# A wider key-value product, earlier squares and reordered attention steps in a two-block transformer kernel

## The chip, the cores and the metric

The kernel runs on one core of a Trainium2 chip. The metric is the device time of one execution in microseconds (us), the median of several runs. The engines are PE (TensorE, the matmuls), PEld (its weight loads), DVE (VectorE), ACT (ScalarE), POOL (GpSimd) and SP (SyncE, which issues nearly all transfers).

## What is computed

Two transformer blocks over 256 tokens of 1024 features, all in float32. The first block mixes a gated linear attention (gla), a windowed pool and a block attention (moba), and has a feed-forward layer. The second has a feed-forward layer, a mixer, a cross attention on a memory and a second feed-forward layer. The change touches the first projection of block one and the mixer of block two:

```
proj = rmsnorm(x) @ w_in                        # block one: q, k (qk), v (gv), the gate input g1, ...
# block two, the mixer: fox attention, and NSA attention = cmp + sel + win
blocks = concat(chunks[:, i:i+nc]) + pos        # cmp: 15 blocks of 32 tokens, stride 16, per group (2) and k / v
k_cmp, v_cmp = gelu(flat(blocks) @ w1) @ w2     # 2048 -> 256 -> 64
o = g0*softmax(q k_cmp) v_cmp + g1*softmax(q k_sel) v_sel + g2*softmax(q k_win) v_win
```

## The kernel before

**Units.** All weights come from one flat array in units of at most 128 x 1024 numbers (512 KB). A chunk is a group of columns of a weight; 512 columns give 4 units of two k-tiles of 128 rows, 256 columns give 2 units of four k-tiles, and g1 with its 16 columns is one small unit. For each unit SP fetches raw (4 buffers, `fetch`), ACT rounds it to fp32r (`whi`, L1262), DVE forms the remainder (`wlo`, L1598), and PE multiplies three ways (hi*hi, lo*hi, hi*lo), 24 matmuls of 256 columns or 12 of 512. SP fetches unit u+4 when the remainder of unit u is done. A product takes its output banks from a ring of four PSUM banks when its first unit starts, and each must have been copied out by its last user; a second ring of four serves the small work. qk takes two banks, g1 one, gv two, and kv one.

**The order.** `order()` writes one plan that every engine walks through: units with their splits two units ahead (AHEAD), the ends of products (the copy out of PSUM), and the steps of tasks. After each unit there is a tick, in which every running task does one step on each engine. STEPS says how many steps a task has, THEN which task starts when another has so many steps left: sel when fox has 0 left, win when sel has 2 left. `drain` gives ticks with no unit between them, and only while the named tasks still run.

**The opening.** SP issues xT0, unit 0, xT1, unit 1, xT2, unit 2, xT3, unit 3, then the two halves of x (by tokens). ACT and DVE split the feature tiles (quarter0_n) and the units. The squares of x (squares0_0 and squares0_1, one for each half of the columns) feed the root (task rest0: sums, a power on POOL, four small DVE operations, and three ticks later `across`, which spreads the root over the partitions by a matmul and a DVE copy, rT). The ends of qk (`kept`, the two halves of gqk) and of g1 (`few`, g1T) need rT.

**The mixer of block two.** The products run qf, gf, vf, kf, kv, qn, ksw, vsw, gg0 to gg3, up10, up11, up00, up01. fox is spawned after kf, cmp after kv. fox, sel and win share `together()`, with ten steps: PE does scores (steps 1 to 3), transposes of the first token block at step 5, values(0) at step 6, the transposes of the second block (7, 8) and values(1) (9). DVE takes the peaks (1 to 3), normalises block 0 (4), at step 5 copies a bank of the transposes (`copied(0, 4)`) and normalises half of block 1, and so on. ACT has the exponentials and the other copies. moba in block one runs through the same function.

For cmp, `out_kv` at the end of kv scales the one bank [k | v] into the SBUF tile kvs. Two transfers (`across_halves`, 128 KB in all) write it with its partition halves swapped into kvx. `rows_of` then makes the tiles R[0] and R[1] (128 partitions x 16 x 32: two tokens of a block stand on the two halves of the partitions) with 8 additions of 64x240, in DVE's first three cmp steps. PE multiplies R[i] with w1 in `first_layer(i)`, L1054, at cmp's third and fourth step.

Of the kernel before, what the change touches and what calls it, by code (L numbers as in the profile page):

```python
# [11 lines left out]
ALU = mybir.AluOpType  # L12
# [5 lines left out]
T = 256  # L18
D = 1024
# [13 lines left out]
def weight_chunks():  # L33
# [16 lines left out]
    for name, a, b in (("gv", 512, 1024), ("g1", 1024, 1040), ("gr", 1040, 1552),  # L50
                       ("pu", 1552, 2064), ("mq", 2064, 2576), ("mk", 2576, 3088), ("mv", 3088, 3600)):
        add(name, "w_in", _cols((a, b)), D)
# [19 lines left out]
    add("kv", w, _cols((512, 768)), D)  # L72
# [217 lines left out]
STEPS = {"gla": 25, "pool": 5, "moba": 13, "fox": 10, "decay": 1, "cmp": 11, "sel": 10, "win": 10, "mixed_first": 1, "mixed_second": 1, "rel": 8, "memory": 16, "w1": 13,  # L290
# [11 lines left out]
THEN = {"fox": ("sel", 0), "sel": ("win", 2)}  # L302


def order(chunks, n_units):
# [9 lines left out]
    def tick():  # L315
        for name in list(left):
            yield "step", name, 0, 0
            left[name] -= 1
            n, ahead = THEN.get(name, (None, 0))
            if n and left[name] == ahead:  # L320
                spawn(n)
            if not left[name]:
                del left[name]

# [56 lines left out]

    yield from do("begin")
# [3 lines left out]
    yield from product("qk", {0: lambda: do("quarter0_3"), 1: lambda: do("squares0_0"), 2: x_squared}, open_end=True)  # L386
    yield from product("gv")
    yield "end", "qk", 0, 0
    yield from product("g1")
# [57 lines left out]
    yield from do("recall")  # L447
    yield from product("up11")
    yield from drain("cmp", "sel", "win")
# [22 lines left out]
def build(nc, io):  # L472
    with ExitStack() as ctx:
# [134 lines left out]
        kvs, kvx = m2.new("kvs", [128, 2, T]), m2.new("kvx", [128, 2, T])  # L608
# [69 lines left out]
        land["kvx"] = Landing(sem("l_kvx"), 2)  # L678
# [122 lines left out]
        def tensor(q):  # L801
# [243 lines left out]
            def cmp():  # L1045
                def first_layer(i):

                    s = ps.take("small", "cmp1", i)
                    q.wait_ge(*ps.empty("cmp1", i))
                    q.wait_ge(*land[f"w1{i}"].at())  # L1050
                    q.wait_ge(*kv_v.at("rows", i))
                    for j in range(0, 16, 4):
                        for g in range(4):
                            r = e.matmul(s[32 * g:32 * g + 32, 0:256], R[i][:, j + g, :], w1[i][:, j + g, :],  # L1054
                                         start=j == 0, stop=j == 12, tile_position=(0, 32 * g))
                    r.then_inc(*ps.filled("cmp1", i))
# [12 lines left out]
                yield  # L1069
                yield  # L1070
# [183 lines left out]
        def scalar(q):  # L1254
# [195 lines left out]
            def cmp():  # L1450
# [9 lines left out]
                yield  # L1460
                yield
# [129 lines left out]
        def vector(q):  # L1591
# [288 lines left out]
            def together(name, ready):  # L1880
# [76 lines left out]
                yield  # L1957
                if name == "sel":
                    q.wait_ge(*ps.full("cmp", "values", 1))
                copied(0, 4)  # L1960
                normalise(1, 0, slice(0, 2), 1, 0)
# [15 lines left out]
            def cmp():  # L1977
                rows_of(0, 0)
                yield
                rows_of(0, 1).then_inc(*kv_v.did("rows", 0))  # L1980
                yield
                for swapped in range(2):
                    r = rows_of(1, swapped)
                r.then_inc(*kv_v.did("rows", 1))
# [90 lines left out]
            def out_kv():  # L2075
                e.tensor_reduce(folding[:, :], ident.rearrange("p (g c) -> p c g", g=4), AX, ALU.add).then_inc(*nsa_v.did("folding"))
                for i in range(2):
                    e.memset(R[i][:, :, 30:32], 0.0)
                q.wait_ge(*used.at(ends["kv"]))
                q.wait_ge(*ps.out("across", 3))  # L2080
                e.tensor_tensor(kvs[:, :, :], ps.tile("kv", 0)[:, :].rearrange("p (i t) -> p i t", i=2), norms[3].wide(),
                                ALU.mult).then_inc(*ps.emptied("kv", 0))

            def rows_of(i, swapped):


                if swapped:
                    q.wait_ge(*land["kvx"].at())
                else:
                    q.wait_ge(*ps.out("kv", 0))  # L2090
                    q.wait_ge(*ps.out("pos"))
                for g in range(2):
                    half_ = 1 - g if swapped else g
                    pa = slice(64 * half_, 64 * half_ + 64)
                    src = (kvx if swapped else kvs)[pa, i, half_:half_ + 1]
                    windows = bass.AP(tensor=src.tensor, offset=src.offset, ap=[list(src.ap[0]), [2, 16], [16, 15]])
                    pt = posT[pa, i, :].unsqueeze(2).to_broadcast([64, 16, 15])
                    r = e.tensor_tensor(R[i][pa, :, 15 * g:15 * g + 15], windows, pt, ALU.add)
                return r
# [167 lines left out]
        def sync(q):  # L2267
# [62 lines left out]
            def across_halves():  # L2330
                q.wait_ge(*ps.out("kv", 0))
                for a, b in ((0, 64), (64, 0)):
                    load("kvx", kvx[a:a + 64, :, :], kvs[b:b + 64, :, :])
                for _ in range(10):
                    yield

# [52 lines left out]
            for i in range(4):  # L2389
                load(f"xT{i}", xT[:, 2 * i:2 * i + 2, :], io["xT"][:, 2 * i:2 * i + 2, :])  # L2390
                fetch(i)
            for t in range(2):
                load(f"x{t}", x[:, t, :], xin[:, t, :])
            load("wg2", wg2[0:16, :], io["gla_w_g2"].rearrange("a r c -> (a r) c"))
# [4 lines left out]
                tasks={"memory": memory, "moba": moba, "rel": rel_bias, "cmp": across_halves, "w1": load_w1})  # L2399
# [74 lines left out]
```

## Time and profile before

| | |
|---|---|
| median of 3 runs | 1122.28 us (1122.17 to 1125.47) |
| profiled execution | 1122.28 us, span 1120.5 us |
| PE busy | 1096.8 us, 98% of the span |
| DVE / ACT busy | 717.4 / 555.6 us |
| mean granted TensorE clock | 0.995 of full speed |
| moved by DMA | 210 MB |

The span is what the trace covers; 1.8 us of the time lie around it. In the trace a matmul's duration is modelled and overlaps the next one, so the distance of two starts is what a matmul costs. Brackets at the end of a row give the idle time of the engine before it and what ended it. L and a number is a line of the kernel.

### The profile page before, as it was taken

What the parts mean: (1) busy time and instruction counts of PE and PEld (TensorE: products, weight loads), DVE (VectorE), ACT (ScalarE), POOL (GpSimd) and SP (SyncE); (2) the same over time, 40 slices, a digit from 0 to 9 for tenths busy, and PEclk for the clock granted to TensorE, in tenths of its full rate; (3) what the DMA queues carried; (4) which work ended last, traced back from release to release, by engine and by line L of the source; (5) the groups of instructions that cost most, each with busy time, mean ns of one, the idle gap of its engine ahead of it and who ended that gap; (6) DMA issues with size and microseconds to landing.
All of it is one profiled execution on the core that took longest, in us unless ns stands there. A gap on an engine that the chain in (4) does not pass through costs nothing.

```text
span 1120.5 us, 18219 instructions
## 1 busy us (share of the span) xinstructions
PE 1096.8 (98%) x7562; PEld 986.0 (88%) x7562; DVE 717.4 (64%) x1074; ACT 555.6 (50%) x836; POOL 22.9 (2%) x43
## 2 busy tenths in 40 slices
PE   8999999999999999999999999999999999999996
PEld 8888778789999988899998899887788989999985
DVE  5686765867666645656676555767676657666653
ACT  6543575545444444544444446446645446445442
POOL 0000400000000000000000000000000000000000
PEclk9999999999999999999999999999999999999998
DMA  7544445554655655676686468233365435665661
GB/s 279 208 154 168 169 160 189 214 197 165 202 189 189 222 197 183 201 242 210 239 269 218 175 209 289 100 114 125 113 236 165 152 128 177 195 199 191 208 201 57
DMA packets 63245, 210.00 MB, mean 187 GB/s; under 512 B 7387, under 2 KB 14731, under 8 KB 62268
## 3 DMA queue, kind: packets, MB, share of 16 engines
q1 hardware_dynamic: 62876, 208.75, 55.0%
q8 instruction: 60, 0.98, 0.4%
q14 instruction: 21, 0.17, 0.0%
q10 hardware_dynamic: 288, 0.10, 0.0%
HBM read 205.39 MB, written 5.26 MB: 188 GB/s over the span
## 4 chain that ended last, share of the span: by engine, by line
PE 83%; DVE 8%; ACT 3%; issue 3%; DMA 1%; POOL 1%; SPq 0%; POOLq 0%; DVEq 0%; ACTq 0%
PE ps L835 13%; PE ps L837 13%; PE ps L838 13%; PE ps L827 12%; PE ps L829 12%; PE ps L828 12%; DVE wlo L1598 2%; PE ps L856 1%; DMA raw<-in_wflat 1%; PE ps L992 1%; DVE wlo_b L1598 1%; PE ps L978 1%; ACT whi L1262 1%; PE ps L903 1%; PE ps L1186 1%
## 5 line engine op out<-in xcount | busy, mean ns | idle before, releaser
L835 PE MATMUL ps<-hT_hi,whi_b 128*128 128x256 f32 x1376 | 383.2, 278 | 3.3 <-DVE wlo_b L1598 3.3
L837 PE MATMUL ps<-hT_hi,wlo_b 128*128 128x256 f32 x1376 | 380.4, 276 | 0.0
L838 PE MATMUL ps<-hT_lo,whi_b 128*128 128x256 f32 x1376 | 380.3, 276 | 0.0
L1598 DVE TENSOR_TENSOR wlo_b<-raw,whi_b 128x1024 fp32r<-128x1024 f32 (+1 forms) x182 | 217.1, 1212 | 109.5 <-ACT whi_b L1262 109.3
L1598 DVE TENSOR_TENSOR wlo<-raw,whi 128x1024 fp32r<-128x1024 f32 x176 | 212.5, 1224 | 116.2 <-ACT whi L1262 115.6
L835 PEld LDWEIGHTS ps<-hT_hi,whi_b 128*128 128x128 f32 x1376 | 258.7, 188 | 6.9 <-issue 5.0
L837 PEld LDWEIGHTS ps<-hT_hi,wlo_b 128*128 128x128 f32 x1376 | 258.8, 188 | 0.3
L838 PEld LDWEIGHTS ps<-hT_lo,whi_b 128*128 128x128 f32 x1376 | 258.6, 188 | 0.0
L1262 ACT ACTIVATE whi<-raw 128x1024 fp32r<-128x1024 f32 x176 | 182.0, 1056 | 112.5 <-PE ps L829 90.3
L1262 ACT ACTIVATE whi_b<-raw 128x1024 fp32r<-128x1024 f32 (+1 forms) x182 | 182.6, 1042 | 34.4 <-PE ps L829 15.5
L827 PE MATMUL ps<-whi,hT_hi 128*128 128x512 f32 (+1 forms) x256 | 101.8, 398 | 2.3 <-DVE wlo L1598 2.3
L827 PE MATMUL ps<-whi,f_hid_hi 128*128 128x512 f32 x264 | 102.8, 389 | 0.0
L828 PE MATMUL ps<-wlo,f_hid_hi 128*128 128x512 f32 x264 | 102.7, 389 | 0.0
L829 PE MATMUL ps<-whi,f_hid_lo 128*128 128x512 f32 x264 | 102.7, 389 | 0.0
L829 PE MATMUL ps<-whi,hT_lo 128*128 128x512 f32 (+1 forms) x256 | 98.2, 384 | 0.0
L828 PE MATMUL ps<-wlo,hT_hi 128*128 128x512 f32 (+1 forms) x256 | 98.2, 384 | 0.0
L1332 ACT ACTIVATE f_sg<-f_sg 128x512 f32<-128x512 f32 x33 | 20.9, 633 | 123.9 <-DVE f_sg L1741 123.9
L827 PEld LDWEIGHTS ps<-whi,hT_hi 128*128 128x128 f32 x256 | 48.1, 188 | 15.8 <-issue 3.9
L829 PEld LDWEIGHTS ps<-whi,f_hid_lo 128*128 128x128 f32 x264 | 49.6, 188 | 10.4
L827 PEld LDWEIGHTS ps<-whi,f_hid_hi 128*128 128x128 f32 x264 | 49.6, 188 | 10.2
L828 PEld LDWEIGHTS ps<-wlo,f_hid_hi 128*128 128x128 f32 x264 | 49.6, 188 | 10.1
L829 PEld LDWEIGHTS ps<-whi,hT_lo 128*128 128x128 f32 x256 | 48.1, 188 | 9.8
(324 smaller groups left out, 1263.0 us busy)
## 6 DMA issues: line engine op xcount, KB each, us to landing
raw<-in_wflat SPq DMA_DIRECT2D x356, 512.0 KB, 4.0
wide<-scratch SPq DMA_DIRECT2D x1, 2048.0 KB, 9.6
m_w<-in_cmp_k_w SPq DMA_DIRECT2D x4, 512.0 KB, 6.7
m_w<-in_cmp_v_w SPq DMA_DIRECT2D x4, 512.0 KB, 6.5
m_alibi<-in_c_alibi SPq DMA_DIRECT2D x1, 1536.0 KB, 7.3
m_xT<-in_xT SPq DMA_DIRECT2D x4, 256.0 KB, 6.6
x<-in_x SPq DMA_DIRECT2D x2, 512.0 KB, 9.8
m_memT<-in_memT SPq DMA_DIRECT2D x1, 1024.0 KB, 5.7
```

What stands on the lines that cost most here:

```text
L827: e.matmul(o, xh, hi[:, k, :], start=first and k == 0, stop=False)
L828: e.matmul(o, xh, lo[:, k, :], start=False, stop=False)
L829: r = e.matmul(o, xl, hi[:, k, :], start=False, stop=last and k == kt - 1)
L835: e.matmul(o, hi[:, k, c], xs.h(k0 + k), start=first and k == 0 and f % 2 == 0, stop=False, skip_group_check=True)
L837: e.matmul(o, lo[:, k, c], xs.h(k0 + k), start=False, stop=False, skip_group_check=True)
L838: r = e.matmul(o, hi[:, k, c], xs.l(k0 + k), start=False, stop=last and k == kt - 1, skip_group_check=True)
L856: r = e.transpose(s[:, 256 * i + 128 * t:256 * i + 128 * t + 128], src(t)[:, 128 * (f + i):128 * (f + i) + 128], ident)
L903: r = e.matmul(ss[par][:, 128 * i:128 * i + 128], kk, qq, start=True, stop=True)
L978: r = e.transpose(s[:, 128 * i:128 * i + 128], Ps[qb][:, h, 128 * k:128 * k + 128], ident)
L1262: e.activation(slot(whi, u)[:, 0:k * n], raw[u % NRAW][:, 0:k * n], ACT.Copy).then_inc(*w_hi.did(u))
L1332: e.activation(b, b, ACT.Silu).then_inc(*silu.did(i, c))
L1598: e.tensor_tensor(slot(wlo, u)[:, 0:k * n], r, h.bitcast(F32), ALU.subtract).then_inc(*w_lo.did(u))
```

## The change

- The opening: SP issues the halves of x before xT3 and unit 3. squares0_0 stands before the split of the last feature tiles, squares0_1 and the root one unit earlier. g1 is multiplied straight after qk and before gv, and the ends of g1 and then qk stand before gv.
- kv: every group of 64 columns is there twice, so kv has 512 columns, 4 units and two banks (k, v), each with both partition halves filled alike. kvs, kvx, the two transfers and rows_of go. out_kv scales each bank in place and makes 16 additions of 64x120 straight from PSUM into R. cmp has 9 steps and not 11, and PE's first layer waits for the end of out_kv's bank.
- `together()` on DVE: in step 5 the normalising comes ahead of the copy.
- win starts when sel is done, and the drain of cmp, sel and win stands before up11.

```diff
     add("qk", "w_in", _cols((256, 512), (0, 256)), D)
-    for name, a, b in (("gv", 512, 1024), ("g1", 1024, 1040), ("gr", 1040, 1552),
+    for name, a, b in (("g1", 1024, 1040), ("gv", 512, 1024), ("gr", 1040, 1552),
...
     for n in range(6):
...
     add("kf", w, _cols((1816, 2328)), D)
-    add("kv", w, _cols((512, 768)), D)
+    add("kv", w, _cols((512, 576), (512, 576), (576, 640), (576, 640),
+                       (640, 704), (640, 704), (704, 768), (704, 768)), D)
...
     add("vsw", w, _cols((896, 1024), (1152, 1280)), D)
...
-STEPS = {"gla": 25, "pool": 5, "moba": 13, "fox": 10, "decay": 1, "cmp": 11, "sel": 10, "win": 10, "mixed_first": 1, "mixed_second": 1, "rel": 8, "memory": 16, "w1": 13,
+STEPS = {"gla": 25, "pool": 5, "moba": 13, "fox": 10, "decay": 1, "cmp": 9, "sel": 10, "win": 10, "mixed_first": 1, "mixed_second": 1, "rel": 8, "memory": 16, "w1": 13,
...
     STEPS[f"rest{_i}"] = 4
...
-THEN = {"fox": ("sel", 0), "sel": ("win", 2)}
+THEN = {"fox": ("sel",), "sel": ("win",)}
...
 def order(chunks, n_units):
...
             left[name] -= 1
-            n, ahead = THEN.get(name, (None, 0))
-            if n and left[name] == ahead:
-                spawn(n)
...
                 del left[name]
+                for n in THEN.get(name, ()):
+                    spawn(n)
...
         names = names or tuple(left)
...
+    def more_x():
+        yield from do("squares0_0")
+        yield from do("quarter0_3")
...
         yield from split_to(n)
-    yield from product("qk", {0: lambda: do("quarter0_3"), 1: lambda: do("squares0_0"), 2: x_squared}, open_end=True)
+    yield from product("qk", {0: more_x, 1: x_squared}, open_end=True)
+    yield from product("g1")
+    yield "end", "qk", 0, 0
     yield from product("gv")
-    yield "end", "qk", 0, 0
-    yield from product("g1")
...
     for name in ("gr", "pu", "mq", "mk", "mv"):
...
     yield from do("recall")
+    yield from drain("cmp", "sel", "win")
     yield from product("up11")
-    yield from drain("cmp", "sel", "win")
...
     yield from product("up01")
...
         onsa = m2.new("onsa", [128, 4, T])
-        kvs, kvx = m2.new("kvs", [128, 2, T]), m2.new("kvx", [128, 2, T])
...
         folding = m2.new("folding", [128, 32], off=whi[1][2].manual_sbuf_range[1])
...
             "cv_out", "ck", "cv")}
-        land["kvx"] = Landing(sem("l_kvx"), 2)
...
                     q.wait_ge(*land[f"w1{i}"].at())
-                    q.wait_ge(*kv_v.at("rows", i))
+                    q.wait_ge(*ps.out("kv", i))
...
                             r = e.matmul(s[32 * g:32 * g + 32, 0:256], R[i][:, j + g, :], w1[i][:, j + g, :],
...
-                yield
-                yield
...
                 first_layer(1)
...
-                yield
-                yield
...
                 gelu(0)
...
                 yield
+                normalise(1, 0, slice(0, 2), 1, 0)
...
                 copied(0, 4)
-                normalise(1, 0, slice(0, 2), 1, 0)
...
                 yield
...
             def cmp():
-                rows_of(0, 0)
-                yield
-                rows_of(0, 1).then_inc(*kv_v.did("rows", 0))
-                yield
-                for swapped in range(2):
-                    r = rows_of(1, swapped)
-                r.then_inc(*kv_v.did("rows", 1))
...
                 s = ps.tile("cmp2")
...
                     e.memset(R[i][:, :, 30:32], 0.0)
-                q.wait_ge(*used.at(ends["kv"]))
-                q.wait_ge(*ps.out("across", 3))
-                e.tensor_tensor(kvs[:, :, :], ps.tile("kv", 0)[:, :].rearrange("p (i t) -> p i t", i=2), norms[3].wide(),
-                                ALU.mult).then_inc(*ps.emptied("kv", 0))
-
-            def rows_of(i, swapped):
...
-
-                if swapped:
-                    q.wait_ge(*land["kvx"].at())
-                else:
-                    q.wait_ge(*ps.out("kv", 0))
+                    s = ps.tile("kv", i)
+                    p2 = s[:, :].rearrange("p (i t) -> p i t", i=2)
+                    q.wait_ge(*used.at(ends["kv"]))
+                    q.wait_ge(*ps.out("across", 3))
+                    e.tensor_tensor(p2, p2, norms[3].wide(), ALU.mult).then_inc(*kv_v.did(i))
+                    q.wait_ge(*kv_v.at(i))
                     q.wait_ge(*ps.out("pos"))
-                for g in range(2):
-                    half_ = 1 - g if swapped else g
-                    pa = slice(64 * half_, 64 * half_ + 64)
-                    src = (kvx if swapped else kvs)[pa, i, half_:half_ + 1]
-                    windows = bass.AP(tensor=src.tensor, offset=src.offset, ap=[list(src.ap[0]), [2, 16], [16, 15]])
-                    pt = posT[pa, i, :].unsqueeze(2).to_broadcast([64, 16, 15])
-                    r = e.tensor_tensor(R[i][pa, :, 15 * g:15 * g + 15], windows, pt, ALU.add)
-                return r
+                    for g in range(2):
+                        for half_ in range(2):
+                            pa = slice(64 * half_, 64 * half_ + 64)
+                            src = s[pa, 256 * g + half_:256 * g + 256:2].rearrange("p (c j) -> p j c", j=8)
+                            for top in range(2):
+                                o = R[i][pa, 8 * top:8 * top + 8, 15 * g:15 * g + 15]
+                                pt = posT[pa, i, 8 * top:8 * top + 8].unsqueeze(2).to_broadcast([64, 8, 15])
+                                r = e.tensor_tensor(o, src[:, :, top:top + 15], pt, ALU.add)
+                    r.then_inc(*ps.emptied("kv", i))
...
                 p2 = ps.tile("ksw", 0)[:, :].rearrange("p (i t) -> p i t", i=2)
...
-            def across_halves():
-                q.wait_ge(*ps.out("kv", 0))
-                for a, b in ((0, 64), (64, 0)):
-                    load("kvx", kvx[a:a + 64, :, :], kvs[b:b + 64, :, :])
-                for _ in range(10):
-                    yield
...
                 for i, n in enumerate(("cmp_k_w1_2", "cmp_v_w1_2")):
...
             oo = io["out"].rearrange("a (k p) d -> p (a k) d", p=128)
-            for i in range(4):
+            for i in range(3):
...
                 load(f"x{t}", x[:, t, :], xin[:, t, :])
+            load("xT3", xT[:, 6:8, :], io["xT"][:, 6:8, :])
+            fetch(3)
...
                             "end": end},
-                tasks={"memory": memory, "moba": moba, "rel": rel_bias, "cmp": across_halves, "w1": load_w1})
+                tasks={"memory": memory, "moba": moba, "rel": rel_bias, "w1": load_w1})
...
         for program in (tensor, scalar, vector, gpsimd, sync):
```

## Rows read from the trace of the kernel before

**Rows 1.** The page, parts 1 and 5: busy time, and the splits of units.

```profile
PE 1096.8 (98%) x7562; PEld 986.0 (88%) x7562; DVE 717.4 (64%) x1074; ACT 555.6 (50%) x836; POOL 22.9 (2%) x43
...
L1598 DVE TENSOR_TENSOR wlo<-raw,whi 128x1024 fp32r<-128x1024 f32 x176 | 212.5, 1224 | 116.2 <-ACT whi L1262 115.6
...
L1262 ACT ACTIVATE whi<-raw 128x1024 fp32r<-128x1024 f32 x176 | 182.0, 1056 | 112.5 <-PE ps L829 90.3
```

**Rows 2.** The page, part 4: the chain that ended last, by engine.

```profile
PE 83%; DVE 8%; ACT 3%; issue 3%; DMA 1%; POOL 1%; SPq 0%; POOLq 0%; DVEq 0%; ACTq 0%
```

**Rows 3.** Stretches: length, busy time by engine, granted clock, DMA share, GB/s.

```profile
9.00:20.00 11.00, 10.99 (x96) 10.79 (x95) 6.48 (x10) 8.03 (x15) 0.00 (x0) 1.00 1.02 402
20.00:36.00 16.00, 15.12 (x79) 12.15 (x80) 9.03 (x17) 7.93 (x12) 0.90 (x2) 1.00 0.52 178
695.00:825.00 130.00, 128.33 (x978) 107.01 (x978) 88.81 (x219) 72.10 (x161) 0.00 (x0) 0.99 0.39 130
702.00:704.00 2.00, 2.00 (x12) 1.78 (x10) 1.43 (x13) 0.00 (x0) 0.00 (x0) 0.50 0.00 0
```

**Rows 4.** PE's timeline inside a unit of qn: start, length.

```profile
717.91 0.28 PE L835 MATMUL ps<-hT_hi,whi_b 128*128 128x256 f32 x1
...
720.51 0.28 PE L838 MATMUL ps<-hT_lo,whi_b 128*128 128x256 f32 x1
```

**Rows 5.** DVE's timeline around the end of kv and cmp's scores.

```profile
710.84 0.38 DVE L2076 TENSOR_REDUCE m_folding<-cst 128x32 f32<-128x128 f32 x1
...
711.23 0.65 DVE L2081 TENSOR_TENSOR m_kvs<-ps,rT 128x512 f32<-128x512 f32 x1
...
716.79 1.16 DVE L2098 TENSOR_TENSOR m_R<-m_kvs,m_posT 64x240 f32<-64x240 f32 x2
...
719.34 1.22 DVE L1922 TENSOR_TENSOR m_P0f<-m_P0f,sm 128x1024 f32<-128x1024 f32 x1
...
746.28 0.30 DVE L2004 TENSOR_TENSOR m_Pc<-ps,m_rel 128x28 f32<-128x28 f32 x2 [4.57 <-PE ps L1102]
...
747.07 0.41 DVE L2004 TENSOR_TENSOR m_Pc<-ps,m_rel 128x60 f32<-128x60 f32 x2
```

**Rows 6.** PE's timeline: cmp's first layer and fox's values.

```profile
721.89 1.93 PE L1054 MATMUL ps<-m_w,m_R 128*32 128x256 f32 x32 [0.18 <-DVE m_R L2098]
...
726.74 1.09 PE L992 MATMUL ps<-m_PT0f,m_vf 128*64 128x128 f32 x16
```

**Rows 7.** Timelines of PE and DVE in win.

```profile
792.91 1.13 PE L1139 MATMUL ps<-m_ksw,m_qn 64*128 64x256 f32 x8 [0.92 <-DVE m_onsa L1936]
...
806.66 0.68 DVE L1926 COPY m_PcT<-ps 128x512 f32<-128x512 f32 x1
...
807.49 1.09 PE L992 MATMUL ps<-m_PcT,m_vsw 128*64 128x128 f32 x16
```

**Rows 8.** ACT's timeline in the opening.

```profile
15.67 0.63 ACT L1287 ACTIVATE junk<-x 128x512 f32<-128x512 f32 x1 [1.61 <-DMA x<-in_x]
```

**Rows 9.** DVE's timeline in the opening.

```profile
20.71 0.16 DVE L1634 TENSOR_TENSOR stat<-stat 128x2 f32<-128x2 f32 x1 [0.21 <-ACT junk L1287]
...
22.57 0.16 DVE L1628 TENSOR_TENSOR stat<-stat,sm 128x2 f32<-128x2 f32 x1
...
27.43 0.42 DVE L1647 COPY rT<-ps 128x256 f32<-128x256 f32 x1 [0.89 <-PE ps L870]
...
29.36 1.28 DVE L1662 SCALAR_TENSOR_TENSOR m_gqk<-ps,rT 128x512 f32<-128x512 f32 x2
```

**Rows 10.** PE's timeline in the opening.

```profile
20.55 0.50 PE L827 MATMUL ps<-whi,hT_hi 128*128 128x512 f32 x1 [0.56 <-DVE wlo L1598]
...
26.78 0.60 PE L870 MATMUL ps<-diag,ones 128*128 128x128 f32 x4
...
35.43 0.40 PE L827 MATMUL ps<-whi,hT_hi 128*128 128x512 f32 x1
```

## The prediction

> **What bounds the kernel now.** I read the page's engine totals first: PE is busy for 1096.8 of 1120.5 us, DVE for 64% and ACT for 50% [rows 1]. The chain that ended last says the same from the other side: 83% of it is PE, and DMA is 1% [rows 2]. Then I looked for PE's idle time where the change lies: 0.89 us in 9 to 36 us, the opening, and 1.67 us in 695 to 825 us, the second block's attention stretch [rows 3]. So a matmul added anywhere costs its full time, and time taken off DVE, ACT or the DMA queue gains only what PE waits there. At the same clock the change can win back about 2.6 us in these two stretches and no more.
>
> Last I read PE's timeline for the price of a unit. Two matmuls of 128x256 that are 23 issues apart start at 717.91 and 720.51, so one takes 0.113 us (the 0.28 us shown overlaps the next) [rows 4]. A unit is 24 of them, 2.71 us. The sum is made against the profiled execution, 1122.28 us with a span of 1120.5, which is also the median of the three runs.
>
> **The kv product, doubled.** With 512 columns kv is four units of two k-tiles instead of two units of four. That is 48 more matmuls: 48 x 0.113 = **+5.4 us** on PE, which has no room for them. The two further loads of 512 KB (DMA share 0.39 here), the two ACT copies of 1.06 us and the two DVE subtractions of 1.22 us lie beside PE [rows 1, 3].
>
> **The rows of R.** The two SBUF copies (kvx) and the 8 additions of 64x240 go. In their place out_kv scales both banks in PSUM and makes 16 additions of 64x120 at once, at the end of kv and ahead of the next unit's subtraction. All steps of cmp keep their place against fox, since cmp loses its two empty first ticks and kv gains two units: PE still asks for R[0] on the tick of fox's first transposes, only kv ends one tick before and not three. Price of one addition: 240 columns take 0.58 us [rows 5]. Two additions of 28 columns take 0.30 and two of 60 columns 0.41, so half of the long one lies between 0.21 and 0.34 (0.10 fixed and half of the remaining 0.48). I take 0.30.
>
> The Trainium skill ("Advanced Engine Details and Errata", The Read-Write Bubble) states that access latency shows as a bubble between DVE instructions and advises large tiles, which speaks against this edit. Its fixed part would put the price at the upper value, 0.34, and this term 0.6 us higher; the trace agrees that there is a fixed part, about 0.10 us.
>
> Now the places in time, on the clock of before (there qn's second unit is PE's work to 717.8; after the change it is kv's fourth). DVE makes fox's normalise from 718.0 to 719.3 (before it stood 1.3 us later, behind the first additions and a subtraction [rows 5]). Then folding 0.38, R's edge 0.06, scale 0.65, eight additions 2.4: bank 0 is out at 722.8. PE has finished fox's transposes at about 721.75, where before it waited 0.18 us for R [rows 6]: it now waits 1.05 us. DVE goes on with bank 1 (3.15 us, to 725.95), the late subtraction (1.15), and then the reordered tick: normalise of 1.4 us with its reciprocal ahead of the copy of 0.65, so PT is there at 729.15. PE gets to fox's values at 727.6 (before: 726.74, without a wait [rows 6]) and waits 1.45 us. After that PE has its first layer, 1.9 us, to itself and DVE catches up. Together 2.5 less the 0.2 of before: **+2.3 us**, with 0.21 and 0.34 in place of 0.30 giving +1.2 and +3.2.
>
> **The sel and win starts.** sel now begins with vsw and win after sel's last step. 30 ticks (10+10+10) fill kv, qn, ksw, vsw, gg and up10, 30 units; before it was 28 of each. So nothing is left to drain at either place, and moving that line costs nothing. PE's 0.92 us wait at 792.91 for the onsa sum, which came from win's scores needing the bank of sel's values, goes: **-0.9 us** [rows 7].
>
> **Normalise ahead of the copy** (all four attentions). The copy of the turned block now comes 1.4 to 1.6 us later, and PE's values(0) wait for it. In win the copy ran 806.66 to 807.3 and PE started at 807.49, right behind it [rows 7]; the same products surround it after the change, so PE waits **+1.6 us** more. In moba, by the same timeline, the copy ends about 1.5 us before PE asks and PE waits at most 0.1; in sel the tick is now inside gg0, away from the sigmoid's table load that made DVE late, so I take -0.2 with a bound of +1.6. fox is counted above.
>
> **The opening.** SP now issues x ahead of xT3 and the fourth weight unit. x landed at 15.67 [rows 8]; 768 KB less ahead of it, at the 402 GB/s of this stretch [rows 3], makes it 13.7. ACT then squares half 0 (two of 0.63 and their reads, 1.5 us in all), makes feature tiles 6 and 7 (0.9) and the upper part of unit 3 (1.06): 17.2. DVE's lower part (1.22) ends at 18.4. PE wanted unit 3 at 17.05 (four units of 2.71 lead up to gv's start at 20.55, which came some 0.8 us late [rows 10]). Unit 3 runs 18.4 to 21.1. Half 1 of the squares ends at 18.7, the root chain takes 2.0 us as between 20.71 and 22.73 [rows 9], g1's lower part is ready at 21.2, g1 runs to 24.0. Now qk, g1 and gv want five banks of a ring of four: gv's second bank is the one that holds qk's first half, so gv starts only when that is copied out. That needs the broadcast of the root (from PE's 26.78 to the end of rT at 27.85, 1.07 us [rows 9, 10]), g1T (at most rT's 0.42) and one half of gqk (1.28 for two): 24.0 + 1.1 + 0.4 + 0.6 = 26.2. PE idles about 1.6 us of these. Four units of gv end at 37.1; before, gr started at 35.43 [rows 10]. **+1.7 us**. Bounds: if the queue serves x no sooner than before, unit 3 comes 2.0 us later still, +3.7; if ACT and DVE overlap better than I lay them out, only the wait at gv is new, less the 1.3 us of waits that go (0.8 at gv's start and 0.5 in its second unit), +0.3.
>
> **Sum.** 5.4 + 2.3 - 0.9 + 1.6 - 0.2 + 1.7 = +9.9 us, 1132.2 us. All waits are laid end to end here, and a late PE gives DVE time, so I shade this down a little: **1131.8 us**.
>
> **Rivals.**
> - *The new waits are mostly covered.* DVE is busy for 88.8 of 130 us in the stretch [rows 3]; if the additions cost 0.21 us, the copy in win is just in time and the opening costs 0.3, then 5.4 + 1.2 - 0.9 + 0 - 0.2 + 0.3 = +5.8: 1128.1. For it: each wait is a difference of two times known to half a microsecond. Against: in win PE stood directly behind the copy.
> - *The clock.* The granted clock was 0.50 in 702 to 704 us, the lower level of 1.2 GHz, and 12 matmuls fit there instead of 18, right after PE multiplied fox's decay with 8 rows in use [rows 3]. The spell of about 3.5 us cost half of itself, 1.75 us. It comes just after kv's first unit, so the change may move it away (1130.1) or, with two further decay groups and new waits in the same stretch, bring a second one: 1133.6, and with sel's bound of +1.6 1135. The Trainium skill ("TensorE: Matmul & The Clock Gate", The HAM clock gate) has these two levels and a fall after idle time; this spell came with PE recorded as busy, so idle time alone does not explain it.
> - *The other side: the tick chain sets the pace.* If the stretch from kf to up10 is bound by the chain fox, sel, win on DVE and ACT, kv's two further units fill time in which PE waits anyway, cmp and fox lose nothing, and only the opening is left: 1124.0, within 0.3%. This decides if PE's idle time in the stretch is over 5.4 us; it is 1.67 [rows 3], some 0.2 more for each wait since modelled ends overhang. An even faster end would need the kvx round trip to have held PE, and its wait on R was 0.18 us.
> - *The edit does not do what it says*: the moved drain is such a line, as shown. The rest of the diff changes what runs.
>
> **How the numbers follow.** A difference of 0.3% (3.4 us) is about what a measurement of this kernel can tell from none. My forecast with all terms near their values (1129 to 1135): 0.60. Mostly covered (1126.5 to 1129): 0.19. Heavier, a second slow spell or several upper bounds (over 1135): 0.14. Other side: 0.07, most of it within 0.3%. The range of 8 in 10 takes in the covered case down to its bulk and the second spell: 1127 to 1136.5. Slower by over 0.3% (above 1125.7): 0.93; same 0.05; faster 0.02.
>
> **What would show it.** 7610 matmuls instead of 7562, and kv as four units. PE waits on DVE by name: about 1.3 us ahead of unit 3 and 1.6 ahead of gv in the opening, gr's first matmul near 37.1; about 1 us ahead of cmp's first layer for R and 1.5 ahead of fox's values; none at win's second scores; 1.6 ahead of win's values(0). PE idle in the attention stretch of about 4 to 5 us in place of 1.67. The prediction is wrong if the additions from PSUM cost under 0.2 or over 0.4 us, if x does not land near 13.7, or if the clock's spell goes or doubles.

## The result, and the profile after

The changed kernel takes **1130.82 us** (median of 4, 1130.05 to 1132.52), the kernel before 1122.22 us on the same chip: a ratio of **1.007**, 95% interval 1.0058 to 1.0083. It is slower by about 8 us, where 1131.8 was forecast. The profiled execution took 1130.39 us with a span of 1128.6.

The page of the changed kernel, parts 1, 4 and 5, against [rows 1, 2]:

```profile
PE 1103.1 (98%) x7610; PEld 993.1 (88%) x7610; DVE 720.9 (64%) x1085; ACT 557.2 (49%) x838; POOL 22.8 (2%) x43
...
PE 83%; DVE 8%; ACT 3%; DMA 3%; issue 1%; POOL 0%; SPq 0%; DVEq 0%; POOLq 0%; ACTq 0%
...
L1596 DVE TENSOR_TENSOR wlo<-raw,whi 128x1024 fp32r<-128x1024 f32 x176 | 212.5, 1224 | 116.1 <-ACT whi L1262 115.4
```

There are 48 matmuls more and PE is busy for 6.3 us more. The rest of the loss must be idle time of PE or a lower clock. The stretches that answer to [rows 3] (length, busy time of PE, PEld, DVE, ACT and POOL, granted clock, DMA share, GB/s):

```profile
9.00:20.00 11.00, 10.42 (x91) 10.26 (x91) 6.71 (x15) 7.92 (x17) 0.90 (x2) 1.00 0.97 367
20.00:36.00 16.00, 14.37 (x81) 11.93 (x80) 9.49 (x13) 5.30 (x5) 0.00 (x0) 1.00 0.70 216
697.00:833.00 136.00, 133.64 (x1028) 113.04 (x1027) 92.03 (x230) 74.39 (x163) 0.00 (x0) 0.99 0.40 132
714.00:720.00 6.00, 6.00 (x34) 5.23 (x33) 3.93 (x12) 3.08 (x10) 0.00 (x0) 0.72 0.26 86
```

PE idles 2.21 us in the opening (0.89 before) and 2.36 us in the attention stretch (1.67). The last row is of a stretch that stands in no row of before: the clock's spell, which stood at 702 us [rows 3], has moved to 716 us.

**The opening**, PE's timeline with its waits (start, length, instruction, idle time before it and who ended it), and below it that of DVE:

```profile
17.73 0.35 PE L837 MATMUL ps<-hT_hi,whi_b 128*128 128x256 f32 x1 [0.58 <-DVE wlo_b L1596]
...
23.30 0.60 PE L872 MATMUL ps<-diag,ones 128*128 128x128 f32 x4
25.53 0.50 PE L829 MATMUL ps<-whi,hT_hi 128*128 128x512 f32 x1 [1.63 <-DVE m_gqk L1660]
...
36.55 0.39 PE L829 MATMUL ps<-whi,hT_hi 128*128 128x512 f32 x1
```

```profile
23.94 0.42 DVE L1645 COPY rT<-ps 128x256 f32<-128x256 f32 x1 [1.20 <-PE ps L872]
24.47 0.41 DVE L1667 TENSOR_TENSOR m_g1T<-ps,rT 16x256 f32<-16x256 f32 x1
24.81 1.27 DVE L1660 SCALAR_TENSOR_TENSOR m_gqk<-ps,rT 128x512 f32<-128x512 f32 x2
```

gv waits for its second bank until DVE has the broadcast root, g1T and half of gqk: 1.63 us. gr starts at 36.55 and not 35.43 [rows 10], **+1.1 us**.

**The end of kv**, DVE's timeline, against [rows 5], and PE's waits there and in win, against [rows 6, 7]:

```profile
718.95 1.23 DVE L1920 TENSOR_TENSOR m_P0f<-m_P0f,sm 128x1024 f32<-128x1024 f32 x1
720.09 0.39 DVE L2067 TENSOR_REDUCE m_folding<-cst 128x32 f32<-128x128 f32 x1
...
720.50 0.70 DVE L2074 TENSOR_TENSOR ps<-ps,rT 128x512 f32<-128x512 f32 x1
721.23 1.94 DVE L2084 TENSOR_TENSOR m_R<-ps,m_posT 64x120 f32<-64x120 f32 x8
...
724.08 1.94 DVE L2084 TENSOR_TENSOR m_R<-ps,m_posT 64x120 f32<-64x120 f32 x8
...
727.40 1.23 DVE L1920 TENSOR_TENSOR m_Pb<-m_Pb,sm 128x1024 f32<-128x1024 f32 x1
728.65 0.69 DVE L1924 COPY m_PT0f<-ps 128x512 f32<-128x512 f32 x1
```

```profile
724.01 1.93 PE L1056 MATMUL ps<-m_w,m_R 128*32 128x256 f32 x32
...
729.49 1.10 PE L994 MATMUL ps<-m_PT0f,m_vf 128*64 128x128 f32 x16 [0.57 <-DVE m_PT0f L1924]
...
815.90 1.09 PE L994 MATMUL ps<-m_PcT,m_vsw 128*64 128x128 f32 x16 [1.66 <-DVE m_PcT L1924]
```

Eight additions take 1.94 us, 0.24 each. No wait for R stands here: PE had the slow spell just ahead of it and came late itself (after_old_opening below, without a spell, shows the wait). win's values wait 1.66 us; the 0.92 us ahead of win's second scores is gone.

To compare stretches I use two marks in PE's timeline: fox's first product with m_fx, and the first transposes of y, which end the mixer. Both kernels' marks:

```profile
698.54 0.48 PE L1039 MATMUL ps<-m_fx,m_sel 8*128 8x128 f32 x2
...
837.75 0.52 PE L856 MATMUL ps<-cst,m_y 128*128 128x128 f32 x3 [0.21 <-DVE m_y L1703]
```

```profile
700.87 0.82 PE L1041 MATMUL ps<-m_fx,m_sel 8*128 8x128 f32 x5
...
845.84 0.41 PE L858 MATMUL ps<-cst,m_y 128*128 128x128 f32 x2 [0.21 <-DVE m_y L1701]
```

The way from fox to y took 139.21 us before and takes 144.97 us now, +5.76. Behind y nothing changed. Of the 2.33 us by which fox starts later, 1.1 are the opening's; the rest arose near 563 us and is taken up in the last section.

### The profile page after: what moved, and what is told of

It is laid out like the page before. It is cut to its first block, busy times and chain, and to the rows that moved or that the text cites. A ratio compares the mean times of both kernels' runs of the same rounds, so it can differ in the third digit from the quotient of the medians.

```text
span 1128.6 us, 18330 instructions
## 1 busy us (share of the span) xinstructions
PE 1103.1 (98%) x7610; PEld 993.1 (88%) x7610; DVE 720.9 (64%) x1085; ACT 557.2 (49%) x838; POOL 22.8 (2%) x43
## 4 chain that ended last, share of the span: by engine, by line
PE 83%; DVE 8%; ACT 3%; DMA 3%; issue 1%; POOL 0%; SPq 0%; DVEq 0%; POOLq 0%; ACTq 0%
PE ps L837 13%; PE ps L839 13%; PE ps L840 13%; PE ps L829 12%; PE ps L831 12%; PE ps L830 12%; DMA raw<-in_wflat 2%; DVE wlo_b L1596 1%; DVE wlo L1596 1%; PE ps L994 1%; PE ps L858 1%; PE ps L980 1%; DMA x<-in_x 1%; ACT whi_b L1262 1%; PE ps L905 1%
## 5 line engine op out<-in xcount | busy, mean ns | idle before, releaser
L837 PE MATMUL ps<-hT_hi,whi_b 128*128 128x256 f32 x1392 | 388.4, 279 | 3.8 <-DVE wlo_b L1596 3.8
L839 PE MATMUL ps<-hT_hi,wlo_b 128*128 128x256 f32 x1392 | 385.4, 277 | 0.0
L840 PE MATMUL ps<-hT_lo,whi_b 128*128 128x256 f32 x1392 | 385.3, 277 | 0.0
L1596 DVE TENSOR_TENSOR wlo_b<-raw,whi_b 128x1024 fp32r<-128x1024 f32 (+1 forms) x184 | 219.6, 1212 | 113.6 <-ACT whi_b L1262 113.4
L837 PEld LDWEIGHTS ps<-hT_hi,whi_b 128*128 128x128 f32 x1392 | 262.1, 188 | 7.9 <-issue 5.2
L839 PEld LDWEIGHTS ps<-hT_hi,wlo_b 128*128 128x128 f32 x1392 | 262.2, 188 | 0.3
L840 PEld LDWEIGHTS ps<-hT_lo,whi_b 128*128 128x128 f32 x1392 | 262.1, 188 | 0.0
## 6 DMA issues: line engine op xcount, KB each, us to landing
wide<-scratch SPq DMA_DIRECT2D x1, 2048.0 KB, 10.7
```

The costliest lines, as they stand in the source:

```text
L837: e.matmul(o, hi[:, k, c], xs.h(k0 + k), start=first and k == 0 and f % 2 == 0, stop=False, skip_group_check=True)
L839: e.matmul(o, lo[:, k, c], xs.h(k0 + k), start=False, stop=False, skip_group_check=True)
L840: r = e.matmul(o, hi[:, k, c], xs.l(k0 + k), start=False, stop=last and k == kt - 1, skip_group_check=True)
L1596: e.tensor_tensor(slot(wlo, u)[:, 0:k * n], r, h.bitcast(F32), ALU.subtract).then_inc(*w_lo.did(u))
```

## The experiments

They ran in two sets of four, each set on one chip beside the kernel before, which had a median of 1122.22 us (17 runs) beside the first set and 1122.64 us (24 runs) beside the second; the row of after has the runs of the result above. "Fox to y" is the distance of the two marks in the profiled execution, and the waits are PE's, without the 0.21 us at the second mark that all have. The spell is the stretch of about 3.5 us at half clock. Waits are named where a bracket shows them; shorter ones follow in the section on the prediction.

| label | median us | ratio (95%) | fox to y | spell in it | waits in it |
|---|---|---|---|---|---|
| before | 1122.22 | 1 | 139.21 | yes | R 0.18, win scores 0.92 |
| after | 1130.82 | 1.007 (1.0058 to 1.0083) | 144.97 | yes | fox values 0.57, win values 1.66 |
| after_copy_first | 1127.39 | 1.0045 (1.0031 to 1.0059) | 143.08 | yes | none |
| after_old_opening | 1129.18 | 1.006 (1.0047 to 1.0073) | 144.95 | no | R 0.78, fox values 1.29, win values 1.66 |
| before_kv_wide | 1129.06 | 1.0058 (1.0045 to 1.0072) | 144.21 | no | R 0.78, win scores 0.92, win transposes 1.39 |
| before_win_late | 1125.06 | 1.0028 (1.0019 to 1.0036) | 140.39 | yes | R 0.18, win transposes 2.39 |
| kv_two_products | 1129.17 (1 run) | | 144.59 | yes | R 1.69, fox values 1.29, win values 1.66 |
| x_first_alone | 1122.51 | 1.0 (0.999 to 1.001) | 137.63 | no | R 0.19, win scores 0.92 |
| sel_sum_early | 1122.17 | 0.9989 (0.9978 to 1.0) | 136.66 | no | R 0.18 |
| kv_wide_win_late | 1127.17 | 1.0033 (1.0021 to 1.0045) | 142.33 | no | R 0.78 |

**after_copy_first**: the changed kernel with the old order in `together()` on DVE.

```diff
                 yield
-                normalise(1, 0, slice(0, 2), 1, 0)
...
                 copied(0, 4)
+                normalise(1, 0, slice(0, 2), 1, 0)
```

> The changed kernel with one edit undone: in the attention steps DVE again copies the turned block before it normalises. My theory: PE's wait ahead of win's values(0) (1.66 us in the changed kernel's trace) falls to about 0.2, the one ahead of fox's values(0) (0.57) goes too, and nothing else moves: 1.8 to 2.2 us less than the changed kernel, about +6.0 us against the kernel before. Rival: the order is free since DVE has slack, and PE then waits for normalised rows one step later: within 0.5 us of the changed kernel.

It took 1127.39 us, 3.4 less than the changed kernel's median and so more than expected. Both profiled executions have a spell in the same place, and the way from fox to y is 1.89 us shorter, inside the 1.8 to 2.2 expected: the waits of 0.57 and 1.66 us are gone, and no wait with a bracket came in their place. Two further kernels differ by this edit alone and have no spell, after_old_opening and kv_wide_win_late: 144.95 and 142.33 us, 2.6 us for the new order. It is a plain loss.

**after_old_opening**: the changed kernel with the opening of before, in the plan and on SP's queue.

```diff
-    for name, a, b in (("g1", 1024, 1040), ("gv", 512, 1024), ("gr", 1040, 1552),
+    for name, a, b in (("gv", 512, 1024), ("g1", 1024, 1040), ("gr", 1040, 1552),
...
-    yield from product("qk", {0: more_x, 1: x_squared}, open_end=True)
-    yield from product("g1")
-    yield "end", "qk", 0, 0
+    yield from product("qk", {0: lambda: do("quarter0_3"), 1: lambda: do("squares0_0"), 2: x_squared}, open_end=True)
     yield from product("gv")
+    yield "end", "qk", 0, 0
+    yield from product("g1")
...
-            load("xT3", xT[:, 6:8, :], io["xT"][:, 6:8, :])
-            fetch(3)
```

> The changed kernel with the opening of the kernel before (transfers, squares, order of qk, gv and g1). My theory: gr's first matmul comes at 35.4 us again and not near 36.5, so the time falls by 1.1 us. Rival: the opening's loss is given back later by an earlier root or gate input, so that the time does not change although gr starts earlier. The wait of about 1.2 us in the first feed-forward layer of block two (near 563 us), which my steps did not have, comes or stays away here for a reason of its own: if it comes from how long the 2 MB transfer of the bias table happens to take, it follows that transfer's time to landing and not this edit.

It took 1129.18 us, 1.6 less by the medians, with intervals that overlap. gr's first matmul is back at 35.26 us. The 2 MB transfer landed after 11.0 us here, and PE waited 0.45 us behind it at 565 us: that wait follows the transfer, as the expectation had it, and the last section has all ten executions. Its profile says more on another matter, since no slow spell fell into the attention stretch. PE's timeline there:

```profile
721.44 1.93 PE L1052 MATMUL ps<-m_w,m_R 128*32 128x256 f32 x32 [0.78 <-DVE m_R L2080]
...
727.61 0.66 PE L990 MATMUL ps<-m_PT0f,m_vf 128*64 128x128 f32 x8 [1.29 <-DVE m_PT0f L1920]
...
814.02 1.09 PE L990 MATMUL ps<-m_PcT,m_vsw 128*64 128x128 f32 x16 [1.66 <-DVE m_PcT L1920]
```

Here both forecast waits stand, 0.78 for R and 1.29 for fox's values, 2.07 us together. The changed kernel's own profile shows 0.57, and its way from fox to y is as long to 0.02 us. So in these two executions the spell and the waits hid each other. It is not so everywhere: in the kernel before, whose wait for R is 0.18 us, the spell costs 1.6 us (139.21 us with it, 137.63 in x_first_alone without).

**before_kv_wide**: the kernel before with the kv part alone (wide kv, no kvx, R from PSUM, nine steps of cmp). win still starts two steps early.

```diff
-    add("kv", w, _cols((512, 768)), D)
+    add("kv", w, _cols((512, 576), (512, 576), (576, 640), (576, 640),
+                       (640, 704), (640, 704), (704, 768), (704, 768)), D)
```

> The kernel before with the kv part of the change alone: 512 columns, four units, additions straight from PSUM, cmp with 9 steps; old opening, old order in the attention steps, win two steps ahead of sel's end. My theory: 48 matmuls of 0.113 us are 5.4 us, and the waits for R and fox's values add at most 0.5 us: +5.4 to +6.0 us. Since cmp and the early win now overlap other products, PE's 0.9 us wait at win's second scores stays. Rival: the block of 16 additions on DVE costs PE another 2 us (as my prediction had it): +7.5 us.

This part alone has most of the loss: 1129.06 us, ratio 1.0058, that is 6.5 us by the ratio and between the two forecasts. The wait for R is 0.78 us as in after_old_opening (at most 0.5 was expected), and one that neither forecast had appears in win, whose steps now fall on other units:

```profile
721.62 1.93 PE L1053 MATMUL ps<-m_w,m_R 128*32 128x256 f32 x32 [0.78 <-DVE m_R L2081]
...
792.11 1.13 PE L1136 MATMUL ps<-m_ksw,m_qn 64*128 64x256 f32 x8 [0.92 <-DVE m_onsa L1931]
804.31 1.09 PE L977 MATMUL ps<-cst,m_P 128*128 128x128 f32 x8 [1.39 <-DVE m_P L1917]
```

**before_win_late**: the kernel before with win started at sel's end.

```diff
-THEN = {"fox": ("sel", 0), "sel": ("win", 2)}
+THEN = {"fox": ("sel", 0), "sel": ("win", 0)}
```

> The kernel before with one edit: win starts when sel has no step left, not two. My theory: PE's wait of 0.92 us at win's second scores goes, and as win now ends with up11 instead of up10, a wait for the last remainder of onsa may stand ahead of up00, up to 1.5 us: between -1.0 and +0.6 us. Rival: win's later end has no cover at all and costs a whole chain of two ticks, +3 us or more.

The 0.92 us wait goes, and one of 2.39 us takes its place: PE's transposes of win's first block, kept by DVE's normalise, which stood behind a late split. Below it, the stretches around that wait:

```profile
808.16 0.69 PE L978 MATMUL ps<-cst,m_P 128*128 128x128 f32 x2 [2.39 <-DVE m_P L1922]
```

```profile
806.00:808.00 2.00, 0.00 (x0) 0.00 (x0) 1.93 (x4) 2.00 (x7) 0.00 (x0) 0.95 0.30 33
808.00:810.00 2.00, 1.84 (x9) 1.84 (x10) 1.33 (x2) 0.87 (x3) 0.00 (x0) 0.50 0.59 229
```

After PE's pause the granted clock is 0.50, the level of 1.2 GHz. The median is 2.8 us above before. So the forecast (-1.0 to +0.6) missed, and the rival's +3 is nearer. The waits explain 1.5 of the 2.8 (2.39 - 0.92); the wait that the forecast allowed ahead of up00 does not come. The profiled execution is the fastest of the 11 (1122.42 us), so its trace does not hold the rest. The mean granted clock of the 11 runs is 0.9955, that of before's 17 is 0.9967, which by itself is 1.3 us of 1120. That this pause draws a spell in most executions would fit, but is not shown, since only one was profiled.

**kv_two_products**: the changed kernel without the product of the remainder of w with the high part of h in kv's four units, so k_cmp and v_cmp are less exact.

```diff
-                            e.matmul(o, lo[:, k, c], xs.h(k0 + k), start=False, stop=False, skip_group_check=True)
+                            if name != "kv":
+                                e.matmul(o, lo[:, k, c], xs.h(k0 + k), start=False, stop=False, skip_group_check=True)
```

> The kernel after, in which kv's four units leave out the product of the remainder of w with the high part of h (32 matmuls fewer; k_cmp and v_cmp are less exact for it). Theory: PE is the bound there, so a matmul of 256 columns costs 0.113 us and the way from fox's first product to the second block's y transposes gets 32 x 0.113 = 3.6 us shorter than the 144.97 us of after, at the same clock: about 141.4. Rival (DVE and ACT set the pace in this stretch, and waits take the place of the matmuls): less than 2 us shorter.

kv's first unit stands ahead of the first mark, so only 24 of the 32 matmuls lie in the stretch, 24 x 0.113 = 2.7 us; the expectation counted one unit too many. PE's timeline from one fox score to the next, over one unit of kv:

```profile
706.77 1.99 PE L1042 MATMUL ps<-m_fx,m_sel 8*128 8x256 f32 x8
708.69 1.13 PE L1038 MATMUL ps<-m_kf,m_qf 64*128 64x256 f32 x8
...
711.79 1.99 PE L1042 MATMUL ps<-m_fx,m_sel 8*128 8x256 f32 x8
...
722.17 1.93 PE L1057 MATMUL ps<-m_w,m_R 128*32 128x256 f32 x32 [1.69 <-DVE m_R L2085]
```

That tick takes 5.02 us; in after_old_opening, with all 24 matmuls, its two starts are 705.09 and 711.04, 5.95 us apart. The 8 matmuls less give 0.93, 0.116 each. PE is the bound inside that tick. But the wait for R grows from 0.78 to 1.69 us, so 0.9 of the 2.7 us is lost again one step later. The 144.59 us measured are 144.95 (after_old_opening) - 2.7 + 0.9 + 1.7 for this run's spell, to 0.3 us. As a number the forecast of 141.4 us missed by 3.2, and the rival's (less than 2 us shorter) holds: against after's 144.97 it is 0.4 us. Two things were left out, the wait behind kv, and that after's spell hid waits while this one, at 702 us, came too early to hide any.

**x_first_alone**: the kernel before with x transferred and squared earlier, and g1 still behind gv.

```diff
+    def more_x():
+        yield from do("squares0_0")
+        yield from do("quarter0_3")
...
-    yield from product("qk", {0: lambda: do("quarter0_3"), 1: lambda: do("squares0_0"), 2: x_squared}, open_end=True)
+    yield from product("qk", {0: more_x, 1: x_squared}, open_end=True)
     yield from product("gv")
```

> The kernel before with only the transfers and squares of x moved: x ahead of xT3 and the fourth weight unit, squares0_0 ahead of the last feature tiles, the rest one unit earlier; g1 stays behind gv, as before. Theory: the loss of the opening lies in g1 and its ends standing ahead of gv, so here the time stays within -0.6 to +0.3 us of before, with at most a wait of 0.6 us ahead of unit 3 in place of those of 0.6 and 0.4 us at gv. Rival (x ahead of the weights is what costs): 0.8 us or more slower, with PE waiting for the fourth unit.

1122.51 us, ratio 1.0. Its waits in the opening:

```profile
18.11 0.36 PE L839 MATMUL ps<-hT_hi,whi_b 128*128 128x256 f32 x1 [0.78 <-DVE wlo_b L1602]
21.39 0.50 PE L831 MATMUL ps<-whi,hT_hi 128*128 128x512 f32 x1 [0.28 <-DVE wlo L1602]
```

The wait ahead of unit 3 is 0.78 and not at most 0.6 us, but 1.06 us of waits in all stand where before had 0.89 (0.56 and 0.33). gr starts at 35.62 us. The same old opening in six executions had it at 34.76 (before_win_late), 35.26, 35.43, 35.59, 35.97 and 36.19 us (kv_wide_win_late, where PE waited 1.33 us for gv's first unit), so 35.62 is no change. With the new opening it is 36.38 to 36.56 us in three. Moving x is free within that spread; what costs in the opening is g1 and its ends ahead of gv, with the 1.63 us for a bank.

**sel_sum_early**: the kernel before with DVE's last sum of sel one step earlier.

```diff
                 copied(1, 12)
                 yield
+                if name == "sel":
+                    result(1)
                 yield
-                result(1)
+                if name != "sel":
+                    result(1)
```

> The kernel before, with DVE's last sum of sel one step earlier, in step 9 behind the last copy, instead of step 10. Theory: win's second scores wait 0.92 us for the bank that this sum empties; a tick earlier it is out in time, and the wait goes: 0.9 us less than before, about 1121.3, with the clock's spell (1.7 us) in the same place. Rival (the sum now holds DVE where PE needs it, ahead of the values, or PE has not finished values(1) and DVE waits): no gain, or a wait of the same size elsewhere.

The wait of 0.92 us is gone. This run and x_first_alone both have no spell in the stretch, and their ways from fox to y are 136.66 and 137.63 us: 0.97 us for one wait of 0.92. The ratio to before is 0.9989 (0.9978 to 1.0), 1.2 us, and its interval ends at 1.0: the gain is shown by the trace, and by the times only as likely. The spell expected in the same place did not come in this execution.

**kv_wide_win_late**: the changed kernel with the old opening and with the copy ahead of the normalising (the two diffs above together). What is left is the wide kv and the later start of win.

> The kernel after with the old opening and with the copy ahead of the normalising: what is left is the wide kv and the later start of win. Theory: 5.4 us for 48 matmuls, about 1 us of waits for R and fox's values, none at win's second scores and none at win's values; from fox's first product to the y transposes 142.9 to 143.3 us without a spell of the lower clock (139.21 in before with one), and the time 5.4 to 6.0 us above before. Rival (win's late start costs the same as its early one, elsewhere): 145 us or more.

1127.17 us, ratio 1.0033, and 142.33 us from fox to y with R's 0.78 as the only wait. Against before_kv_wide, which starts win two steps earlier, it is 1.9 us faster: the waits of 0.92 and 1.39 us are both gone. So the late start gains 2.3 us of waits beside the wide kv and loses 1.5 us without it. Both the 142.9 to 143.3 us and the 5.4 to 6.0 us above before were expected too high (142.33 us; +4.5 by the medians, +3.7 by the ratio). The 48 matmuls are not the reason: they cost 5.6 us here, but short pauses of before in sel are gone (next section).

## Why the prediction was right

The place of every wait in the sum was right, and no term was off by more than 0.6 us. The column "measured" compares two executions without a spell in the attention stretch, after_old_opening and x_first_alone, which holds the kernel before from kv on: 144.95 - 137.63 = +7.3 us. A wait is measured here as the distance of PE's two starts, less the distance that the same two steps have without a wait.

| term | forecast | measured |
|---|---|---|
| kv's 48 matmuls | +5.4 | +5.5 |
| R and fox's values | +2.3 | +2.0 |
| win's second scores | -0.9 | -1.0 |
| win's values and second transposes | +1.6 | +1.3 |
| sel | -0.2 | -0.5 |
| opening | +1.7 | +1.1 |
| sum | +9.9, shaded to +9.5 | +8.4; medians +8.6, ratio +7.9 |

- **kv, and four short pauses.** The kernel before has four waits in sel and win that are too short for a bracket: 0.10 to 0.14 us of idle time ahead of the first values and of the second block's transposes, 0.2 to 0.3 us each from start to start. They wait for DVE's copy or normalise. PE's timeline at the first of them, in x_first_alone and then, without the pause, in after_old_opening:

```profile
773.78 0.39 PE L833 MATMUL ps<-whi,hT_lo 128*128 128x512 f32 x1
774.30 1.09 PE L996 MATMUL ps<-m_PcT,m_vsw 128*64 128x128 f32 x16
```

```profile
774.79 0.39 PE L827 MATMUL ps<-whi,hT_lo 128*128 128x512 f32 x1
775.11 1.09 PE L990 MATMUL ps<-m_PcT,m_vsw 128*64 128x128 f32 x16
```

  The distance is 0.52 us in the one and 0.32 in the other. The two pauses in sel are gone in each of the three kernels with the wide kv that ran without a spell, which is the -0.5. With every wait that adds over 0.1 us taken off, long or short, 135.5 us are left from fox to y in x_first_alone and in sel_sum_early, and 141.1, 141.1 and 140.9 in after_old_opening, kv_wide_win_late and before_kv_wide. So the 48 matmuls cost 5.4 to 5.6 us in five executions: their full price, as forecast.
- **R and fox's values.** The step from normalise to copy was right in order and shape. Eight additions took 1.94 us, 0.24 each and not 0.30, inside the bounds of 0.21 to 0.34. By the prediction's own steps 16 additions lie ahead of fox's values, so its bounds of 0.21 and 0.34 give about +0.9 and +2.9 us and not +1.2 and +3.2; at 0.24 they give +1.3, and +2.0 was measured, so a part of this term's nearness is luck. The Trainium skill ("Advanced Engine Details and Errata", The Read-Write Bubble) advises large tiles, which speaks against halving them. The trace does not bear that out as a cost of this edit: two additions of 64x120 from PSUM take 0.48 us, one of 64x240 from SBUF took 0.58 [rows 5]. But the source and its access pattern changed along with the size, so the pair does not test the advice by itself.
- **Normalise ahead of the copy.** In win the bracket shows 1.66 us for a forecast of 1.6, and after_copy_first removes it; the two short pauses of before that it replaces leave +1.3. In sel it costs nothing.
- **The opening.** The chain was right (unit 3, g1, broadcast, g1T, half of gqk, gv), at 25.53 us for a forecast of 26.2. It was mis-sized at its head: ACT had x at 13.10 us and not 13.7 (its first square after the wait for x), and unit 3 started at 17.73 and not 18.4. The +1.1 (36.55 - 35.43) is of one pair of profiles; by the spread of the old opening's executions it could be anything from 0.2 to 1.8.
- **The rival of the other side** (the tick chain sets the pace) is excluded: in kv_wide_win_late PE idles only 1.14 of the 136 us from 697 to 833 (134.86 busy), less than before's 1.67 of 130, and the time still rises by 3.7 us. In one tick of kv_two_products every matmul left out gives back 0.116 us.
- **The clock rival** is half right. The spell moved and did not double; it did change which of the waits can be seen.
- **The signs.** The changed kernel's own profile shows fewer of them than the prediction named: no wait for R where about 1 us was to stand, 0.57 for 1.5 ahead of fox's values, 0.58 for 1.3 ahead of unit 3, and 2.36 us of idle time in the stretch for 4 to 5. after_old_opening has 0.78 and 1.29, and 3.73 us together with win's 1.66. Taken from the one profile alone, the account would have looked worse than it was. All of the misses but the 0.1 us of kv lie on the high side, and the forecast of 1131.8 us is as close as it is partly because the sum was shaded.

## What to carry to other kernels

Where PE is 98% busy, a transfer and a few DVE operations that already lie beside it are worth nothing, and matmuls that replace them cost their full price. When a step moves in a plan of ticks, work out for each bank and each copy who asks for it next: the same later start of win gained 2.3 us of waits in one order and cost 1.5 in the other. Compare two profiles only after their spells of a lower clock are taken out, since a spell can hide the wait behind it, and add up the distances of starts, since a wait too short for a bracket is worth 0.2 to 0.3 us each time.

## What the runs showed of the hardware

- **The clock's spell wanders.** It lasts about 3.5 us at the 1.2 GHz level and costs 1.6 to 1.7 us where it hides no wait. In one execution each it stood at 701 (before), 716 (after), 715 (after_copy_first), 702 (kv_two_products) and 808 us (before_win_late), and in the five others there was none before the kernel's last matmuls. The same stretch of after_copy_first and of kv_wide_win_late, both in kv's units and fox's scores, has 39 matmuls at a clock of 0.72 and 47 at 1.00:

```profile
714.00:720.00 6.00, 6.00 (x39) 5.62 (x38) 4.89 (x15) 3.03 (x9) 0.00 (x0) 0.72 0.25 82
```

```profile
714.00:720.00 6.00, 6.00 (x47) 5.22 (x46) 3.73 (x12) 3.08 (x11) 0.00 (x0) 1.00 0.29 89
```

  Ahead of four of the five falls PE was recorded as busy, and it had multiplied fox's decay, with 8 rows in use, in the 2 us before; ahead of the one at 808 us it stood idle for 2.39 us. The same products stand in the same place in the five executions without a spell, so they are not enough to bring one, and what does stays open. The Trainium skill ("TensorE: Matmul & The Clock Gate", The HAM clock gate) has the fall after idle time; the trace agrees at 808 us, and not in the other four.
- **One long transfer varies.** The 2 MB copy `wide` from DRAM to DRAM landed 9.6 us after its issue in before's profile and 10.7 in after's. SP's queue waits for it, and the weights behind it came later: ACT waited 3.55 us for raw at 561 us, and PE then idled 0.18 and 0.53 us in the feed-forward layer, which before's profile doesn't show. Both lines are ACT's and PE's timelines of the changed kernel:

```profile
561.30 1.06 ACT L1262 ACTIVATE whi_b<-raw 128x1024 fp32r<-128x1024 f32 x1 [3.55 <-DMA raw<-in_wflat]
```

```profile
563.68 0.39 PE L837 MATMUL ps<-hT_hi,whi_b 128*128 128x256 f32 x1 [0.18 <-DVE wlo_b L1596]
...
567.25 0.35 PE L837 MATMUL ps<-hT_hi,whi_b 128*128 128x256 f32 x1 [0.53 <-DVE wlo_b L1596]
```

  The change touches nothing there. after_copy_first, with the same code in that place, landed it after 9.4 us and reached fox 1.0 us earlier than after. Over the ten executions the time to landing is 9.1 to 11.3 us: in the four up to 9.6 us PE has no wait there, in the six from 9.9 on it has 0.15 to 1.15 us. Both groups hold kernels with the old kv and with the wide one (sel_sum_early 9.1 us and no wait, x_first_alone 11.1 us and 0.56). So this part of a single profile's difference is the execution's, not the kernel's.
